# Recurrent heads of a second mixer, run between the weight blocks of its conv panels

## The reference, cut to what matters

```
proj = h @ w_in                                  # 1024 -> 7 x 512
c_gate, hc, b_gate, q, f_pre, v, g = split(proj)
# conv branch
y = b_gate * conv3(c_gate * hc);  y = group_rmsnorm(y, gain, groups of 64)
# recurrent branch, 4 heads of 128, chunks of 32 tokens
f = lb + (1 - lb) * sigmoid(f_pre);  k = 1 - f;  G = cumsum(log f) inside a chunk
q_dec = silu(q) * 128**-0.5 * exp(G);  k_dec = k * exp(-G);  k_end = k * exp(G_last - G)
o = tril(q_dec @ k_dec.T) @ v + q_dec @ state;   state = exp(G_last) * state + k_end.T @ v
o = o * rsqrt(mean(o*o) + EPS) * gain * silu(g)
x = x + concat([conv, o]) @ w_out                # 1024 -> 1024
```

## Time and profile before

| | before |
|---|---|
| median of 3 runs (lowest, highest) | 1847.74 us (1845.44, 1848.54) |
| the profiled execution's own time, and its span | 1845.54 us, 1843.8 us |
| busy PE / DVE / ACT / POOL | 1734.7 / 1176.1 / 950.2 / 129.9 us |
| mean granted clock of TensorE | 0.966 of full |

### The profile page before, as it was taken

The page is one execution under the profiler, slowest core; times in us unless marked ns, Lnnn a source line. Parts: engine busy times, 40 slices in busy tenths (PEclk is TensorE's granted clock), DMA queues, the critical chain, the costliest instruction groups (busy, mean ns, idle before and its releaser), DMA issues.

```text
span 1843.8 us, 30285 instructions
## 1 busy us (share of the span) xinstructions
PE 1734.7 (94%) x10352; PEld 1536.8 (83%) x10352; DVE 1176.1 (64%) x1749; ACT 950.2 (52%) x1536; POOL 129.9 (7%) x108
## 2 busy tenths in 40 slices
PE   8999999998898899989878899989999999999998
PEld 6887898787686688778768899989999988888887
DVE  5554676476463655456655389987888866666664
ACT  5445535475462544346334354546666655555554
POOL 0000004000000000000001002032222200000000
PEclk9999999999898999989979999999999999999999
DMA  7554543342351455545415354544444456666663
GB/s 255 185 186 153 184 159 117 111 139 92 107 190 57 148 183 184 168 137 172 137 56 183 105 172 157 183 158 130 141 141 137 137 172 193 193 193 193 193 193 126
DMA packets 78814, 286.79 MB, mean 156 GB/s; under 512 B 8864, under 2 KB 9120, under 8 KB 78624
## 3 DMA queue, kind: packets, MB, share of 16 engines
q1 hardware_dynamic: 77888, 282.27, 47.5%
q0 software_dynamic: 864, 3.67, 0.7%
HBM read 284.86 MB, written 1.05 MB: 155 GB/s over the span
## 4 chain that ended last, share of the span: by engine, by line
PE 79%; DVE 14%; ACT 5%; issue 2%; DMA 0%; ACTq 0%; SPq 0%; DVEq 0%
PE ps L1591 24%; PE ps L1593 23%; PE ps L1592 23%; DVE w_low L921 4%; PE ps L2095 3%; ACT w_high L460 1%; DVE digit_hot L1486 1%; PE ps L1770 1%; PE ps L1941 1%; DVE xT_low L954 1%; PE ps L1680 1%; PE ps L2060 0%; PE ps L1955 0%; DVE route L1462 0%; PE ps L1823 0%
## 5 line engine op out<-in xcount | busy, mean ns | idle before, releaser
L921 DVE TENSOR_TENSOR w_low<-ring,w_high 128x1024 fp32r<-128x1024 f32 x532 | 653.7, 1232 | 419.7 <-ACT w_high L460 418.3
L460 ACT ACTIVATE w_high<-ring 128x1024 fp32r<-128x1024 f32 x532 | 560.1, 1056 | 384.8 <-PE ps L1593 379.2
L1591 PE MATMUL ps<-xT_high,w_high 128*128 128x256 f32 x1600 | 467.7, 292 | 15.3 <-DVE w_low L921 10.1
L1592 PE MATMUL ps<-xT_high,w_low 128*128 128x256 f32 x1600 | 458.8, 287 | 0.0
L1593 PE MATMUL ps<-xT_low,w_high 128*128 128x256 f32 x1600 | 458.7, 287 | 0.0
L1591 PEld LDWEIGHTS ps<-xT_high,w_high 128*128 128x128 f32 x1600 | 313.5, 196 | 19.4 <-DVE w_low L921 13.1
L1592 PEld LDWEIGHTS ps<-xT_high,w_low 128*128 128x128 f32 x1600 | 313.7, 196 | 1.0 <-issue 1.0
L1593 PEld LDWEIGHTS ps<-xT_low,w_high 128*128 128x128 f32 x1600 | 313.0, 196 | 0.0
L1591 PE MATMUL ps<-w_high,xT_high 128*128 128x512 f32 x480 | 193.7, 403 | 9.7 <-DVE xT_low L954 3.8
L1591 PE MATMUL ps<-w_high,expert_w_high 128*128 128x512 f32 x512 | 199.3, 389 | 0.0
L1592 PE MATMUL ps<-w_high,expert_w_low 128*128 128x512 f32 x512 | 199.2, 389 | 0.0
(11 more groups left out here) (344 smaller groups left out, 2134.3 us busy)
## 6 DMA issues: line engine op xcount, KB each, us to landing
ring<-in_stream SPq DMA_DIRECT2D x532, 512.0 KB, 3.4
row_gain<-in_rows POOLq DMA_DIRECT2D x4, 512.0 KB, 4.5
h<-in_x SPq DMA_DIRECT2D x2, 512.0 KB, 4.1
mem_sb<-in_mem SPq DMA_DIRECT2D x1, 1024.0 KB, 11.4
keys_sb<-in_keys POOLq DMA_DIRECT2D x1, 1024.0 KB, 5.1
out<-result SPq DMA_DIRECT2D x2, 512.0 KB, 2.6
last_gain<-in_rows POOLq DMA_DIRECT2D x1, 512.0 KB, 5.0
cols<-in_cols SPq DMA_DIRECT2D x1, 78.5 KB, 7.3
```

The costliest lines, as they stand in the source:

```text
L460: act.activation(WH[:, n % SLOTS, :], RING[:, n % SLOTS, :], ACT.Copy).then_inc(w_high, 1)
L921: dve.tensor_tensor(WL[:, n % SLOTS, :], RING[:, n % SLOTS, :], WH[:, n % SLOTS, :].bitcast(F32), ALU.subtract).then_inc(w_split, 1)
L1591: pe.matmul(out, high, w_hi, start=start, stop=False, skip_group_check=True)
L1592: pe.matmul(out, low, w_hi, start=False, stop=False, skip_group_check=True)
```

## The change

- In the second mixer PE no longer runs `plain`. It runs `late(n, blocks)`, parts of panels, and between them the steps of the recurrent branch: keys to tokens and scores before the last block of v; the first key-value products inside panel c; the second ones with the first head outputs inside panel hc; the second head outputs and both transposes around and inside panel b. These steps use the upper PSUM banks (columns 2048 to 4095). DVE and ACT get a written-out order (`late_step`, `late_panel` and the steps between them), where `late_step(n)` splits block n + 4 of the stage.
- The product `U = CG * HC` moves from DVE to POOL; each fourth of the conv goes between splits on DVE.
- The rows of `w_out_2` that belong to the heads come first; their operands are `HOH` and `HOL`. The group means of the conv follow after the first of these blocks, and the last conv steps are cut into two halves.
- 1/sqrt(m + EPS) is exp(-0.5 ln(m + EPS)) on ACT for the heads and the conv, in place of an addition and a reciprocal on DVE and a square root on ACT.
- `FUTURE` and `IDENT` are copied once to fp32r, and `row_sums` of the first mixer uses these copies.
- ACT squares tile 0 for the next norm ahead of the splits of two blocks, and not after them.

The diff, indentation cut; of the second mixer's old lists, which the new ones replace, the removed lines are left out:

```diff
@@ -180,6 +180,12 @@
+HO = sb("hg_out", [P, TT, 4, P], 169)
...
+HOH = sb("hg_outT_high", [P, 4, SEQ], 113, F32R)
+HOL = sb("hg_outT_low", [P, 4, SEQ], 153, F32R)
+HOT_PS = PS[:, 2560:3584].rearrange("p (h t) -> p h t", h=4)
@@ -221,6 +227,8 @@
+FUTURE_R = sb("future_r", [P, P], 205, F32R)
+IDENT_R = sb("ident_r", [P, P], 64.5, F32R)
@@ -409,6 +418,9 @@
+    pool.wait_ge(evac_a, EVAC["w_in_2"] + 6)
+    pool.wait_ge(evac_d, EVAC["w_in_2"] + 6)
+    pool.tensor_tensor(U[:], CG, HC, ALU.mult).then_inc(u_ok, 1)
@@ -771,60 +783,100 @@
+    def late_step(n, count=1):
+        split(BASE["w_in_2"] + PB + n, count)
+    def late_panel(n):
+        evac("w_in_2", mixer_dst, n, PAIR[n % 2])
+    def late_out(n):
+        act.wait_ge(evac_a, e + n + 1)
+        act.wait_ge(evac_d, e + n + 1)
+    def head_scale(tt):
+        act.wait_ge(hg_p, 3 + tt)
+        o = PS[:, 3584:4096] if tt == 0 else PS[:, 2048:2560]
+        r, m, q = (STAT[:, c + 4 * tt:c + 4 * tt + 4] for c in (32, 40, 48))
+        for h in range(4):
+            last = act.activation(HSQ[:, h, :], o[:, h * P:(h + 1) * P], ACT.Square, accum_out=r[:, h:h + 1])
+        chain(last)
+        chain(act.activation(m, r, ACT.Ln, scale=1.0 / P, bias=STAT[:, EPS_COL:EPS_COL + 1]))
+        act.activation(q, m, ACT.Exp, scale=-0.5).then_inc(hg_a, 1)
+    late_step(0, 2)
+    act.wait_ge(hg_d, 1)
+    act.activation(LBS[:, 2:4, :], LBS[:, 0:2, :], ACT.Exp).then_inc(hg_a, 1)
+    late_step(2, 2)
+    late_panel(0)
+    late_out(0)
+    act.activation(FG[:], F2, ACT.Sigmoid).then_inc(hg_a, 1)
+    act.preload_act_table_set("natural_log_exp_and_others")
+    late_step(4, 2)
+    act.wait_ge(hg_d, 2)
+    act.activation(GC[:], FG[:], ACT.Ln).then_inc(hg_a, 1)
+    late_step(6, 2)
+    late_panel(1)
+    late_step(8)
+    act.wait_ge(hg_d, 4)
+    act.activation(KEN[:], KEN[:], ACT.Exp).then_inc(hg_a, 1)
+    act.activation(KD[:], GC[:], ACT.Exp, scale=-1.0).then_inc(hg_a, 1)
+    late_step(9)
+    act.activation(EG[:], GC[:], ACT.Exp).then_inc(hg_a, 1)
+    late_step(10, 2)
+    late_panel(2)
+    late_out(1)
+    act.activation(Q2, Q2, ACT.Silu).then_inc(hg_a, 1)
+    late_out(2)
+    act.activation(G2, G2, ACT.Silu).then_inc(hg_a, 1)
+    act.preload_act_table_set("natural_log_exp_and_others")
+    late_step(12, 3)
...
+    act.activation(KE[:].rearrange("p t h n -> p (t h n)"), PS[:, 2048:3072], ACT.Copy).then_inc(hg_a, 1)
+    late_step(15)
+    late_panel(3)
+    late_step(16, 2)
...
+    late_step(18, 2)
+    late_panel(4)
+    late_step(20, 2)
+    head_scale(0)
+    late_step(22, 2)
+    late_panel(5)
+    late_step(24)
+    head_scale(1)
+    late_step(25, 2)
+    act.wait_ge(hg_p, 6)
+    act.activation(HOH[:], HOT_PS, ACT.Copy, scale=COLS[:, HG_GAIN:HG_GAIN + 1]).then_inc(hg_a, 1)
+    late_step(27)
+    late_panel(6)
...
+    b = BASE["w_out_2"] + PB
+    for half in range(2):
+        act.wait_ge(c2_d, half + 1)
+        act.activation(halves(MS, half), halves(Y, half), ACT.Square).then_inc(c2_a, 1)
+    split(b, 1)
+    for half in range(2):
+        act.wait_ge(c2_p, half + 1)
+        m = halves(MS, half).rearrange("p f t -> p (f t)")
+        chain(act.activation(m, PS[:, 1024 + half * 512:1536 + half * 512], ACT.Ln,
+                             bias=STAT[:, EPS_COL:EPS_COL + 1]))
+        act.activation(m, m, ACT.Exp, scale=-0.5).then_inc(c2_a, 1)
+    for half in range(2):
+        act.wait_ge(c2_d, half + 3)
+        act.activation(halves(XTH[:, 4:8, :], half), halves(Y, half), ACT.Copy).then_inc(c2_a, 1)
+        split(b + 1 + half, 1)
...
+    split(b + 3, 1)
...
+    split(b + 4, 2)
@@ -1194,6 +1246,9 @@
+    dve.wait_ge(ident_ok, 1)
+    dve.tensor_copy(FUTURE_R[:], FUTURE[:]).then_inc(future_r, 1)
+    dve.tensor_copy(IDENT_R[:], IDENT[:]).then_inc(future_r, 1)
@@ -1319,97 +1374,129 @@
+    def late_step(n, count=1):
+        split(BASE["w_in_2"] + PB + n, count)
+    def late_panel(n):
+        evac("w_in_2", mixer_dst, n, PAIR[n % 2])
+    def states(n0, n1):
+        for n in range(n0, n1):
+            dve.wait_ge(s_ok, n)
+            for h in range(4):
+                last = dve.scalar_tensor_tensor(
+                    ST2[:, n, h, :], ST2[:, n - 1, h, :], EG[:, h, (n + 1) * HG_CHUNK - 1:(n + 1) * HG_CHUNK],
+                    PS[:, 2048 + n % 4 * 512 + h * P:2048 + n % 4 * 512 + (h + 1) * P], ALU.mult, ALU.add)
+            last.then_inc(s_ok, 1)
+    def head_out(tt):
+        dve.wait_ge(hg_a, 10 + tt)
+        o = PS[:, 3584:4096] if tt == 0 else PS[:, 2048:2560]
+        chain(dve.tensor_tensor(HO[:, tt, :, :], o.rearrange("p (h n) -> p h n", h=4),
+                                STAT[:, 48 + tt * 4:52 + tt * 4].unsqueeze(2).to_broadcast([P, 4, P]), ALU.mult))
+        dve.tensor_tensor(HO[:, tt, :, :], HO[:, tt, :, :], G2[:, tt, :].rearrange("p (h n) -> p h n", h=4),
+                          ALU.mult).then_inc(hg_d, 1)
...
+    late_step(0, 2)
+    dve.wait_ge(hg_a, 1)
...
+    late_step(2, 2)
+    late_panel(0)
+    dve.wait_ge(hg_a, 2)
+    for ft in range(4):
+        last = dve.tensor_scalar(FG[:, ft, :], FG[:, ft, :], LBS[:, 7, ft:ft + 1], LBS[:, 6, ft:ft + 1],
+                                 ALU.mult, ALU.add)
+    last.then_inc(hg_d, 1)
+    dve.wait_ge(hg_d, 2)
+    chain(dve.tensor_scalar(KH[:], FG[:], -1.0, 1.0, ALU.mult, ALU.add))
+    late_step(4, 2)
+    dve.wait_ge(hg_a, 3)
...
+    dve.tensor_tensor_scan(flat, CHUNK_ON[:], flat, 0.0, ALU.mult, ALU.add).then_inc(hg_d, 1)
+    dve.wait_ge(hg_d, 3)
+    dve.tensor_tensor(chunks(KEN), chunks(GC)[:, :, HG_CHUNK - 1:].to_broadcast([P, 32, HG_CHUNK]), chunks(GC),
+                      ALU.subtract).then_inc(hg_d, 1)
+    late_step(6, 2)
+    late_panel(1)
+    late_step(8)
+    dve.wait_ge(hg_a, 4)
+    dve.tensor_tensor(KEN[:], KEN[:], KH[:], ALU.mult).then_inc(hg_d, 1)
+    dve.wait_ge(hg_a, 5)
+    dve.tensor_tensor(KD[:], KD[:], KH[:], ALU.mult).then_inc(hg_d, 1)
+    late_step(9, 3)
+    late_panel(2)
+    dve.wait_ge(hg_a, 7)
+    dve.scalar_tensor_tensor(QD[:], Q2, P ** -0.5, EG[:], ALU.mult, ALU.mult).then_inc(hg_d, 1)
+    late_step(12, 4)
+    late_panel(3)
+    late_step(16)
...
+                                   PS[:, 3072 + tt * 512:3584 + tt * 512].rearrange("p (h n) -> p h n", h=4))
...
+    late_step(17)
+    states(1, 4)
+    late_step(18, 2)
+    late_panel(4)
+    late_step(20, 2)
+    dve.wait_ge(kv_ps, 2)
+    states(4, 7)
+    late_step(22)
+    head_out(0)
+    late_step(23)
+    late_panel(5)
+    late_step(24)
+    dve.wait_ge(u_ok, 1)
+    conv2(0)
+    late_step(25)
+    head_out(1)
+    conv2(1)
+    late_step(26)
+    conv2(2)
+    dve.wait_ge(hg_a, 12)
+    dve.scalar_tensor_tensor(HOL[:], HOT_PS, COLS[:, HG_GAIN:HG_GAIN + 1], HOH[:].bitcast(F32),
+                             ALU.mult, ALU.subtract).then_inc(hg_d, 1)
+    late_step(27)
+    conv2(3)
+    late_panel(6)
...
+    dve.wait_ge(evac_a, EVAC["w_in_2"] + 7)
+    dve.wait_ge(evac_d, EVAC["w_in_2"] + 7)
+    for half in range(2):
+        dve.tensor_tensor(halves(Y, half), halves(Y, half), halves(BG, half), ALU.mult).then_inc(c2_d, 1)
+    split(b, 1)
+    for half in range(2):
+        dve.wait_ge(c2_a, half + 3)
+        for ft in (2 * half, 2 * half + 1):
+            last = dve.scalar_tensor_tensor(Y[:, ft, :], Y[:, ft, :], COLS[:, CONV_GAIN2 + ft:CONV_GAIN2 + ft + 1],
+                                            MS[:, ft, :], ALU.mult, ALU.mult)
+        last.then_inc(c2_d, 1)
+    for half in range(2):
+        dve.wait_ge(c2_a, half + 5)
+        dve.tensor_tensor(halves(XTL[:, 4:8, :], half), halves(Y, half), halves(XTH[:, 4:8, :], half).bitcast(F32),
+                          ALU.subtract).then_inc(c2_d, 1)
+        split(b + 1 + half, 1)
+    split(b + 3, 1)
@@ -1800,13 +1887,14 @@
+        pe.wait_ge(future_r, 2)
...
-            last = pe.matmul(o.rearrange("p (h n) -> p h n", h=4), IDENT[:],
-                             FUTURE[:].unsqueeze(1).to_broadcast([P, 4, P]), start=False, stop=True)
+            last = pe.matmul(o.rearrange("p (h n) -> p h n", h=4), IDENT_R[:],
+                             FUTURE_R[:].unsqueeze(1).to_broadcast([P, 4, P]), start=False, stop=True)
@@ -1966,20 +2054,33 @@
+    def late(n, blocks=range(PB)):
+        if n >= 2 and 0 in blocks:
+            pe.wait_ge(evac_a, EVAC["w_in_2"] + n - 1)
+            pe.wait_ge(evac_d, EVAC["w_in_2"] + n - 1)
+        if n:
+            (panel_tokens if n in (2, 3) else panel_features)(BASE["w_in_2"] + PB * n, PAIR[n % 2], None, blocks)
+        else:
+            panel_features(BASE["w_in_2"], PAIR[0], norm=7)
+    def keys_to_tokens():
+        pe.wait_ge(hg_d, 5)
+        for tt in range(TT):
+            for h in range(4):
+                o = 2048 + (tt * 4 + h) * P
+                last = pe.transpose(PS[:, o:o + P], KEN[:, h, tt * P:(tt + 1) * P], IDENT[:])
+        last.then_inc(hg_p, 1)
+    def chunk_scores():
+        pe.wait_ge(hg_d, 7)
+        for tt in range(TT):
+            for h in range(4):
```

(111 more changed lines are left out.)

107 lines of the change are left out of this document (14 added, 93 removed).

## The result

The changed kernel takes **1818.4 us** (median of 4 runs, 1814.8 to 1822.4) against 1847.8 beside it: ratio 0.985, 95% interval 0.983 to 0.987. The forecast was 1823, range 1817 to 1833.

A forecast was written before the change was run, and what follows sets the result against it. PE, busy 94% of the span, was taken as the bound. Terms -20.3, -4.4, -0.3 and +0.7 sum to -24.3: from 1845.5 to 1821.2 us, with the median 2.2 above, so 1823; range 1817 to 1833.

The forecast's parts named there:

- Parts 1 and 2: Second mixer, last panel b split release to `w_out_2` end: 39.2 us of PE work plus 5.5 of waits against 65.0, -20.3.
- The four large waits: PE's waits for masked scores (0.8 us), tile 1's head outputs (0.9), `HOL` (1.8) and the conv's group means (1.9).
- the fifth: PE's wait for states 4 to 6, which stand behind split 21: 0.1 us.
- worth nothing by itself: Removing the 6.55 us reciprocal and DVE's additions gains nothing alone: under PE's three blocks, with 2.2 us to spare.
- Part 3: Product U on POOL, 1.9 us alone or 2.8 beside DVE: cost 0, at worst 2.8 us.
- Part 4: First mixer's masks in fp32r: 3.8 to 5.0 us gained, taken as -4.4; bound 0 if fp32r brought nothing.
- Part 5: At the end, tile 0 is squared while tile 1 is multiplied: 0 to -3 us, taken as -0.3.
- The +0.7 for changing between panels and small matmuls: PE changes between panels and small matmuls some ten times more than before: an estimated cost of 0.7 us.
- thin stretches: Rival: PE's clock falls during small work between dense blocks; one to three falls give 1826 to 1831 us; chance 0.32.
- The conv's end: Rival: late conv makes PE wait 10 us around `w_out_2`'s first blocks: 1829, up to 1835 without cover; chance 0.12.
- a sign of being wrong: ACT or DVE showing a wait ahead of a split longer than 6.3 us, the lateness reckoned free.
- Masks that bring nothing: Rival: fp32r masks gain nothing, hidden behind the DVE wait or no faster: 1828 us; chance 0.05.

## Why the prediction was right, and what was mis-sized

- **Parts 1 and 2 (mixer, -20.3): right, and for the reason given.** 65.0 us became 27.4, panels q to b went from 68.6 to 85.7 (85.4 forecast, but the prediction's own terms, 68.6 + 15.3 + 1.8, make 85.7), from the start of panel q to the end of `w_out_2` it is 113.1 for 133.6: -20.5. The four large waits, forecast 0.8, 0.9, 1.8 and 1.9, were 0.95, 1.00, 1.66 and 1.56; the fifth, 0.1 for the states, was 0. The sum had the clock in it only by pricing all work at full clock. The busy column shows how much that was: 9.6 of 21.0 us. That the clock would hold was a chance of 0.46 against 0.32 for its fall, not something that the working had derived.
- **The reciprocal "worth nothing by itself": wrong in the new order, of which it was said.** Undone there it costs 7.0 us. The cover was 2.3 us (2.2 forecast), which the prediction had worked out itself, and the two halves of 4.0 us pass it; 4.7 us of wait and 2.3 of clock are what is left over. The sum was not touched, since it was built from the new order with the logarithms in place. In the old order the roots are worth 0.0. Once the heads lie between the blocks, roots and rows are each worth something without the other (6.2 and 9.9 us).
- **Part 3 (POOL, 0):** right; its product took 2.40 us (897.9 to 900.3) and DVE's form costs 0.4. That POOL and DVE shut each other out of SBUF was not tried: DVE ran nothing from 897.7 to 901.4.
- **Part 4 (masks, -4.4): the mis-sized term.** The work is -5.0 by the timeline and -4.7 to -5.3 with the clock taken out, about the upper bound of 5.0. The part that was to be hidden behind the wait of 1.90 us was not: the wait is still 1.90, since DVE's chain moved forward with PE's result. The other 3.3 us of the 8.3 are the clock ahead of the first mark, for which the sum had no term. So the excess of the gain over the forecast is 1.1 us in the mixer and behind it (-21.0 for -19.9), 0.6 in the masks and 3.3 in the clock. That last part brought the time near 1817, a bound that the prediction had reasoned from vanishing waits; the waits did not vanish.
- **Part 5 (-0.3):** `w_out_2` to `peer_q` took 8.06 us for 8.52, -0.5. The +0.7 for changing between panels and small matmuls did not appear: from 825 to 937 PE is idle for 5.24 us, of which the four waits are 5.17.
- **Rivals.** The clock did not fall in the thin stretches of the new order: 1.00 from 825 to 937, through waits of 1.6 us and a run of 32-row products. It fell from 1.00 in the waits of 4.70 and 6.28 us of other kernels. The conv's end was not late, but the experiment with the reciprocal shows that 2.3 us was all that kept it so. (The rival's upper end of 1835 does not follow from its terms: 1829 and 2.2 more are 1831.) Masks that bring nothing and stalls in strict queues did not happen. ACT did wait 7.22 us ahead of a split, which is over the 6.3 us that the prediction named as a sign of being wrong. But it waited for PE to free a block, behind 5.2 us of thin work, and PE did not wait for that split: the sign mistook an early engine for a late one.

```profile
887.85 1.06 ACT L472 ACTIVATE w_high<-ring 128x1024 fp32r<-128x1024 f32 x1 [7.22 <-PE ps L1680]
```

- **Open.** Kernels with float32 masks lost 23.9 to 27.5 us to the clock ahead of the first mark, those with fp32r masks 17.9 to 24.5. With the timed medians this leans to a loss that is lower with shorter masks, by some 4 us; neither that nor its cause is settled.

## What to carry to other kernels

Price a step by what it leaves uncovered, in the order in which it will stand: the same logarithm roots were worth 0.0 us in the old order and 7.0 in the new. A wait of some us on the busiest engine costs twice, itself and by the clock behind it (9.6 of the 21.0 us here), so its end is worth more than its length. But small work put between dense blocks won only 4.1 us here, all of it clock, while the chain behind it had nothing to cover it; the cover, by the order of the rows and by the cheaper roots, gave 16.9. Where whole times scatter by the clock, compare a stretch between two marks of the program: it told 0.4 us apart where medians could not tell 3.5.
